# Gate and up products of a SwiGLU layer as seven products of half-size blocks

## The chip, the cores and the metric

One core of a Trainium2 chip runs the whole program. The metric is device time in microseconds (us) of one execution; lower is better. TensorE does the matrix products, VectorE (DVE in the profile), ScalarE (ACT) and GpSimd (POOL) the elementwise work, SyncE (SP) issues the loads.

## The reference

Two pre-norm layers over 512 tokens of width 1024 in float32, each followed by a dense SwiGLU feed-forward of width 2816. Layer 0 mixes tokens with windowed attention, layer 1 with latent attention. The feed-forward is what the change concerns:

```python
def _swiglu(h, w_gu, w_down):
    g, u = jnp.split(h @ w_gu, 2, axis=-1)
    return (jax.nn.silu(g) * u) @ w_down

h = h + _swiglu(_rmsnorm(h, norm_ffn[i]), ffn_w_gu[i], ffn_w_down[i])
```

`h @ w_gu` is 512 x 1024 by 1024 x 5632 in each layer. Float32 accuracy is wanted throughout.

## The kernel before

**Data.** The stream lies transposed: `h`, `x_hi`, `x_lo` are 128 partitions x 8 blocks of the width x 512 tokens. To keep float32 accuracy every operand A is split as A = hi + lo, where hi is A rounded to the format `F32R` that TensorE takes, and lo the rest, rounded likewise; a product is three matmuls (`product`: lo·hi, hi·lo, hi·hi) added up in a PSUM bank. x is split once per layer. The weights are split as they arrive: GpSimd writes `w_hi` (`w_split_hi`, L530), VectorE the rest `w_lo` = `w_raw` - `w_hi` (`w_split_lo`, L2330).

**Feed-forward.** It has 22 pairs of a gate block and an up block of 128 columns, in two halves of 11 (`HALF`); each half first makes its 11 pairs of products and the hidden blocks f = silu(gate)·up (`f_hi`, `f_lo`), then runs 8 down blocks of 11 products each, added to `h`. A pair is 2 blocks x 8 width blocks x 3 = 48 matmuls with 512 columns moving. VectorE multiplies gate by the inverse norm `rs_t` (L2666), ScalarE takes silu (L1118), GpSimd multiplies by `rs_t` once more for the up part (L727), VectorE multiplies with up out of PSUM (`hid`, L2681), ScalarE rounds (`f_hi`, L1121), VectorE subtracts (`f_lo`, L2683).

**Order.** It is written out by hand for each engine; semaphores are the only order between engines (`w_ready` for a split weight block, `w_used` for one multiplied, `proj_free` for a bank read). Most pairs run in hardware loops (`Fori`). Weight blocks alternate between two slots, loaded by SyncE (`load`, `load_ffn`).

## Time and profile before

| what | value |
|---|---|
| median of 3 timed runs | 1155.4 us (1154.16 to 1155.7) |
| span of the profiled execution | 1153.3 us |
| TensorE busy | 1141.3 us, 99% of the span |
| VectorE / ScalarE / GpSimd busy | 607.6 / 334.1 / 460.7 us |
| moved by DMA | 97.81 MB, 85 GB/s mean |
| granted clock of TensorE | 0.998 of full, mean |

The profiled execution has no timed value of its own; its span, first to last instruction, is 2.1 us below the median of the timed runs. Busy time of an engine is the time with an instruction in it. Matmuls overlap their neighbours, so the start-to-start distance, not the duration, says what a matmul costs in a row of them. The idle time in square brackets names the engine whose signal ended the wait.

### The profile page before, as it was taken

The numbers are of one execution on the slowest core, as the hardware profiler recorded it, in microseconds if no ns is written. First come the engines' busy times: TensorE is split into PE (matmuls) and PEld (weight loads), VectorE is DVE, ScalarE is ACT, GpSimd is POOL, SyncE is SP. The second block draws the span as 40 slices with busy tenths as digits, with TensorE's granted clock in tenths as the row PEclk, the third lists the DMA queues.
The fourth block names the chain that finished last, engine by engine and source line by source line (L and its number), as shares of the span: only waits on it lengthen the run. The fifth ranks groups of instructions, "written<-read, shape, count | busy, mean of one in ns | idle before, by whom it ended". The sixth has DMA issues, their size and how long they took to land.

```text
span 1153.3 us, 17024 instructions
## 1 busy us (share of the span) xinstructions
PE 1141.3 (99%) x5674; PEld 957.3 (83%) x5674; DVE 607.6 (53%) x1036; ACT 334.1 (29%) x709; POOL 460.7 (40%) x487
## 2 busy tenths in 40 slices
PE   8999999999999999999999999999999999999997
PEld 8877688888888888888998888888888888888886
...
GB/s 193 111 37 38 37 80 99 96 91 94 116 100 74 104 96 91 113 100 97 84 40 39 19 20 37 37 110 92 106 94 98 118 80 87 95 106 91 126 76 73
DMA packets 175362, 97.81 MB, mean 85 GB/s; under 512 B 7880, under 2 KB 171216, under 8 KB 175312
## 3 DMA queue, kind: packets, MB, share of 16 engines
...
## 4 chain that ended last, share of the span: by engine, by line
PE 95%; DVE 2%; ACT 1%; DMA 1%; issue 0%; POOL 0%; SPq 0%; ACTq 0%; DVEq 0%
PE bank L1415 28%; PE bank L1419 28%; PE bank L1418 28%; PE bank L2082 2%; PE bank L2101 1%; PE bank L2104 1%; PE bank L1645 1%; PE bank L1629 1%; PE bank L1660 1%; PE bank L1661 1%; PE bank L2013 1%; DMA w_raw<-in_a_w_qkv 1%; ACT s_a L1006 0%; PE bank L1515 0%; PE bank L1851 0%
## 5 line engine op out<-in xcount | busy, mean ns | idle before, releaser
L2330 DVE TENSOR_TENSOR w_lo<-w_raw,w_hi 128x1024 fp32r<-128x1024 f32 (+3 forms) x139 | 189.2, 1362 | 280.4 <-POOL w_hi L530 280.4
L530 POOL TENSOR_SCALAR w_hi<-w_raw 128x1024 fp32r<-128x1024 f32 (+3 forms) x147 | 166.3, 1131 | 411.6 <-PE bank L1419 401.5
L1415 PE MATMUL bank<-x_hi,w_lo 128*128 128x512 f32 x744 | 290.8, 391 | 0.0
L1419 PE MATMUL bank<-x_hi,w_hi 128*128 128x512 f32 x744 | 289.7, 389 | 0.0
L1418 PE MATMUL bank<-x_lo,w_hi 128*128 128x512 f32 x744 | 289.5, 389 | 0.0
L1419 PEld LDWEIGHTS bank<-x_hi,w_hi 128*128 128x128 f32 x744 | 139.6, 188 | 29.1
L1418 PEld LDWEIGHTS bank<-x_lo,w_hi 128*128 128x128 f32 x744 | 139.7, 188 | 28.9
L1415 PEld LDWEIGHTS bank<-x_hi,w_lo 128*128 128x128 f32 x744 | 139.7, 188 | 28.5
L1415 PE MATMUL bank<-f_hi,w_lo 128*128 128x512 f32 (+1 forms) x363 | 139.7, 385 | 0.0
L1419 PE MATMUL bank<-f_hi,w_hi 128*128 128x512 f32 (+1 forms) x363 | 138.9, 383 | 0.0
L1418 PE MATMUL bank<-f_lo,w_hi 128*128 128x512 f32 (+1 forms) x363 | 138.9, 383 | 0.0
L727 POOL TENSOR_TENSOR gate_s<-gate_s,rs_t 128x512 f32<-128x512 f32 x44 | 56.7, 1288 | 114.2 <-ACT gate_s L1118 114.2
L1118 ACT ACTIVATE gate_s<-gate_t 128x512 f32<-128x512 f32 x44 | 27.8, 631 | 251.9 <-DVE gate_t L2666 251.9
L1121 ACT ACTIVATE f_hi<-hid 128x512 f32 (+1 forms) x44 | 27.8, 632 | 214.1 <-DVE hid L2681 214.1
L2631 DVE TENSOR_TENSOR h<-h,bank 128x512 f32<-128x512 f32 (+1 forms) x40 | 27.5, 688 | 112.5 <-PE bank L1419 109.0
L1418 PEld LDWEIGHTS bank<-f_lo,w_hi 128*128 128x128 f32 x363 | 68.2, 188 | 13.2
L1419 PEld LDWEIGHTS bank<-f_hi,w_hi 128*128 128x128 f32 x363 | 68.2, 188 | 13.3
L1415 PEld LDWEIGHTS bank<-f_hi,w_lo 128*128 128x128 f32 x363 | 68.2, 188 | 13.2
L812 POOL TENSOR_SCALAR s_b<-s_b,stat 128x512 f32<-128x512 f32 x64 | 44.9, 709 | 60.8 <-DVE stat L2624 60.6
L544 POOL TENSOR_TENSOR ss<-ss,sq 128x512 f32<-128x512 f32 x27 | 49.9, 1848 | 32.8 <-ACT sq L924 32.7
L2683 DVE TENSOR_TENSOR f_lo<-hid,f_hi 128x512 f32 (+1 forms) x44 | 30.5, 693 | 42.9 <-ACT f_hi L1121 42.9
L2976 DVE TENSOR_TENSOR bpt_lo<-bank,bpt_hi 128x512 fp32r<-128x512 f32 x64 | 42.5, 683 | 9.3 <-ACT bpt_hi L1248 9.1
...
## 6 DMA issues: line engine op xcount, KB each, us to landing
w_raw<-in_ffn_w_gu SPq DMA_DIRECT2D x88, 512.0 KB, 3.8
...
w_raw<-in_a_w_qkv SPq DMA_DIRECT2D x10, 512.0 KB, 4.6
w_raw<-in_a_w_o SPq DMA_DIRECT2D x8, 512.0 KB, 3.5
w_raw<-in_b_w_o SPq DMA_DIRECT2D x8, 512.0 KB, 3.7
...
x_n<-in_x SPq DMA_DIRECT2D x4, 512.0 KB, 5.6
```

The source lines that it names most:

```text
L530: pool.tensor_scalar(split_part(w_hi, s, cols, kv), raw_part(s, cols, kv), 1.0, 1.0, ALU.mult, ALU.mult) \
L544: pool.tensor_tensor(n.ss[:], n.ss[:], n.sq[:, b, :], ALU.add).then_inc(ss_ready, 1)
L727: pool.tensor_tensor(gate_s[:], gate_s[:], rs_t[:], ALU.mult).then_inc(silu_rs_ready, 1)
L812: pool.tensor_scalar(view, view, stat[:, 2, u % 8:u % 8 + 1], 1.0, ALU.mult, ALU.mult) \
L1118: act.activation(gate_s[:], gate_t[:], ACT.Silu).then_inc(silu_ready, 1)
L1121: act.activation(f_hi[:, j, :], hid[:], ACT.Copy).then_inc(f_hi_ready, 1)
L1415: first = pe.matmul(o, ll, rh, start=start, stop=False)
L1418: pe.matmul(o, lh, rl, start=False, stop=False)
L1419: return pe.matmul(o, lh, rh, start=False, stop=stop)
L2330: dve.tensor_tensor(split_part(w_lo, s, cols, kv), raw_part(s, cols, kv), f(split_part(w_hi, s, cols, kv)), ALU.subtract) \
L2683: dve.tensor_tensor(f_lo[:, j, :], hid[:], f(f_hi[:, j, :]), ALU.subtract).then_inc(f_ready, 1)
L2976: dve.tensor_tensor(bpt_lo[:, hd % 2, i, :], banks[3 + u % 2][:], f(bpt_hi[:, hd % 2, i, :]), ALU.subtract).then_inc(pt_free, 1)
```

## The change

Of the 22 pairs in a layer the first two stay as they were. Each of the other 20 is computed as a 2 x 2 block product: the width of 1024 is cut into two halves of 4 blocks (`HK`), the 512 tokens into two halves of 256 columns (`HT`), and the third division is gate against up. With weight blocks A11, A12 (gate, low and high width), A21, A22 (up) and x blocks X11 (low width, early tokens) and so on, the seven products are Strassen's in Winograd's form:

- weight sums S1 = A21 + A22, S2 = S1 - A11, S3 = A11 - A21, S4 = A12 - S2, made for each pair by GpSimd (`sums_12`, `sums_43`);
- x sums T1 to T4, made once a layer while the attention's output product runs (`t_first`, `t_last`, `t_high`, `t_low`);
- seven products of 4 blocks each, 7 x 4 x 3 = 84 matmuls with 256 columns moving (`seven`), two of them with x itself, twice each over halves, the others with sums.

Sums and blocks are split into hi and lo in four groups: G0 = A11, A12 (1024 columns), G1 = S1, S2 (1024), G2 = A22 (512), G3 = S4, S3 (1024). ScalarE makes the hi parts (`group_hi`), VectorE the lo parts (`group_lo`). The products share banks; ScalarE copies partial results from PSUM to SBUF between them (`take_product`, four a pair, 256 columns each) and TensorE adds later products on top of what stands in the bank (`add_product`). VectorE finishes gate and up with three additions (`late_gate`, `rest_of_unit`); up now lies in SBUF, no longer in PSUM, when `hid` is multiplied. Raw weights of a pair come into one slot of 1 MB (`load_raw`) as two transfers of 512 KB, two such slots alternate. The loops are unrolled. Down products are as before, in the new slots.

```diff
+            def load_raw(layer, c0, r, cols, *parts):
+                if r >= 2:
...
+                        sp.wait_ge(g_ready, 4 * unit_of(past // RAW_LAYER, j) + 4)
...
+                for i, src in enumerate(parts):
...
+                    sp.dma_start(dst, src).then_inc(raw_in[r % 2], 16)
# GpSimd
+            def sums_12(layer, j):
...
+                pool.wait_ge(raw_in[r % 2], raw_landed(r))
+                if u:
+                    pool.wait_ge(g_ready, 4 * (u - 1) + 2)
...
+                pool.tensor_tensor(s12[:, 0:QUART], a21, a22, ALU.add).then_inc(s12_ready, 1)
+                pool.wait_ge(s12_ready, 2 * u + 1)
+                pool.tensor_tensor(s12[:, QUART:2 * QUART], s12[:, 0:QUART], a11, ALU.subtract).then_inc(s12_ready, 1)
+            def sums_43(layer, j):
...
+                if u:
+                    pool.wait_ge(g_ready, 4 * (u - 1) + 4)
+                pool.tensor_tensor(s43[:, QUART:2 * QUART], a11, a21, ALU.subtract).then_inc(s43_ready, 1)
+                pool.wait_ge(s12_ready, 2 * u + 2)
+                pool.tensor_tensor(s43[:, 0:QUART], a12, s12[:, QUART:2 * QUART], ALU.subtract).then_inc(s43_ready, 1)
# ScalarE, each pair j
+                    if j > 2 and j > j0:
+                        take_product(layer, j - 1, 3)
+                    group_hi(layer, j, 3)
+                    take_product(layer, j, 0)
+                    if j > 2 and j > j0:
+                        silu(layer, j - 1)
+                    if j + 1 < j1:
+                        group_hi(layer, j + 1, 0)
+                    take_product(layer, j, 1)
+                    take_product(layer, j, 2)
+                    if j > j0:
+                        f_high(layer, j - 1)
+                    if j + 1 < j1:
+                        group_hi(layer, j + 1, 1)
+                        group_hi(layer, j + 1, 2)
+            def take_product(layer, j, which):
+                if which == 0 and u:
+                    act.wait_ge(c_ready, 3 * u)
+                act.wait_ge(m_done, 7 * u + (1, 3, 4, 7)[which])
# TensorE, each pair
+                pe.wait_ge(g_ready, 4 * u + 1)
+                one(main[:, 0:HT], 0, 0, xs(0, early))
+                one(apart[:, 0:HT], 0, 1, xs(HK, early))
...
+                pe.wait_ge(g_ready, 4 * u + 2)
+                one(side[:, 0:HT], 1, 0, ts(0))
+                pe.wait_ge(m_read, 4 * u + 1)
+                one(main[:, 0:HT], 1, 1, ts(1), start=False)
+                pe.wait_ge(g_ready, 4 * u + 3)
+                one(apart[:, HT:T], 2, 0, ts(3))
+                pe.wait_ge(g_ready, 4 * u + 4)
+                pe.wait_ge(m_read, 4 * u + 2)
+                one(side[:, 0:HT], 3, 0, xs(HK, late), start=False)
+                pe.wait_ge(m_read, 4 * u + 3)
+                one(main[:, 0:HT], 3, 1, ts(2), start=False)
# VectorE
+            def group_lo(layer, j, g):
...
+                dve.wait_ge(g_hi_ready, 4 * u + g + 1)
+                dve.tensor_tensor(G_LO[g], group_raw(r, g), f(G_HI[g]), ALU.subtract).then_inc(g_ready, 1)
+            def late_gate(layer, j):
...
+                dve.tensor_tensor(gate_t[:, HT:T], u2_m5[:, 0:HT], banks[3 * (u % 2) + 1][:, 0:HT], ALU.add) \
+                    .then_inc(c_ready, 1)
+            def rest_of_unit(layer, j):
...
+                dve.tensor_tensor(hid[:, HT:T], m1_u3[:, HT:T], u2_m5[:, HT:T], ALU.add).then_inc(c_ready, 1)
+                dve.tensor_tensor(gate_up[:, :, 0:HT], m1_u3[:].rearrange("p (c n) -> p c n", c=2),
+                                  banks[3 * (u % 2) + 2][:].rearrange("p (c n) -> p c n", c=2), ALU.add) \
+                    .then_inc(c_ready, 1)
+                dve.wait_ge(c_ready, 3 * u + 3)
+                dve.tensor_tensor(gate_t, gate_t, rs_t[:], ALU.mult).then_inc(gate_ready, 1)
```

VectorE, within a half's pairs. Before, one turn of the loop (one pair):

```order
387 L2330 TENSOR_TENSOR w_lo_58<-w_raw_54,w_hi_56 128x1024 [waits w_hi_ready]
388 L2666 TENSOR_TENSOR gate_t<-bank,rs_t 128x512 [waits silu_ready,w_used]
389 L2330 TENSOR_TENSOR w_lo_59<-w_raw_55,w_hi_57 128x1024 [waits w_hi_ready]
390 L2681 TENSOR_TENSOR hid<-bank,gate_s 128x512 [waits f_ready,silu_rs_ready,w_used]
391 L2683 TENSOR_TENSOR f_lo<-hid,f_hi 128x512 [waits f_hi_ready]
```

The changed kernel, one pair at the same place in the second half (`u_m` is `u2_m5`, `m_u` is `m1_u3`, `s_126` is `s12`, `s_127` is `s43`; `gate_up` holds gate and `hid`):

```order
501 L2937 TENSOR_TENSOR x_lo<-s_127,x_hi 128x4x256 [waits g_hi_ready]
502 L2937 TENSOR_TENSOR w_lo_58<-raw_125,w_hi_56 128x1024 [waits g_hi_ready]
503 L2969 TENSOR_TENSOR gate_up<-gate_up,gate_s 128x512 [waits silu_rs_ready]
504 L2974 TENSOR_TENSOR f_lo<-gate_up,f_hi 128x512 [waits f_hi_ready]
505 L2937 TENSOR_TENSOR g_lo<-s_126,g_hi 128x1024 [waits g_hi_ready]
506 L2937 TENSOR_TENSOR w_lo_59<-raw_125,w_hi_57 128x512 [waits g_hi_ready]
507 L2945 TENSOR_TENSOR gate_up<-u_m_123,bank 128x256 [waits silu_ready,m_read,m_done]
508 L2953 TENSOR_TENSOR gate_up<-m_u_122,u_m_123 128x256 [waits f_ready,m_read]
509 L2954 TENSOR_TENSOR gate_up<-m_u_122,bank 128x2x256
510 L2958 TENSOR_TENSOR gate_up<-gate_up,rs_t 128x512 [waits c_ready]
```

Before, three of the five instructions of a pair took both inputs from SBUF (387, 389, 391), the other two took one from a bank. Now eight of ten take both from SBUF, and only rows 507 and 509 take one from a bank. The lo parts of G0, G1 and G2 made here are those of the next pair, that of G3 is this pair's.

GpSimd at the same place. Before:

```order
199 L727 TENSOR_TENSOR gate_s<-gate_s,rs_t 128x512 [waits silu_ready]
200 L530 TENSOR_SCALAR w_hi_57<-w_raw_55 128x1024 [waits w_used,w_in1]
201 L530 TENSOR_SCALAR w_hi_56<-w_raw_54 128x1024 [waits w_used,w_in0]
202 L727 TENSOR_TENSOR gate_s<-gate_s,rs_t 128x512 [waits silu_ready]
203 L530 TENSOR_SCALAR w_hi_57<-w_raw_55 128x1024 [waits w_used,w_in1]
```

The changed kernel, one pair:

```order
404 L835 TENSOR_TENSOR s_126<-raw_121 128x512 [waits g_ready,raw_in0]
405 L837 TENSOR_TENSOR s_126<-s_126,raw_121 128x512 [waits s12_ready]
406 L853 TENSOR_TENSOR gate_s<-gate_s,rs_t 128x512 [waits silu_ready]
407 L846 TENSOR_TENSOR s_127<-raw_121 128x512 [waits g_ready]
408 L848 TENSOR_TENSOR s_127<-raw_121,s_126 128x512 [waits s12_ready]
```

The two roundings of weights have gone to ScalarE, and four sums of two inputs stand in their place; `gate_s` waits behind the first two sums, which wait for the lo part of G1 (row 505 of VectorE).

## Rows read from the trace of the kernel before

**Rows 1.** The page: busy time by engine, then the chain that ended last
```profile
PE 1141.3 (99%) x5674; PEld 957.3 (83%) x5674; DVE 607.6 (53%) x1036; ACT 334.1 (29%) x709; POOL 460.7 (40%) x487
...
PE 95%; DVE 2%; ACT 1%; DMA 1%; issue 0%; POOL 0%; SPq 0%; ACTq 0%; DVEq 0%
```

**Rows 2.** Busy time by stretch: the gate and up products, layer 0, first half
```profile
core 0: us, PE busy (x) PEld busy (x) DVE busy (x) ACT busy (x) POOL busy (x), PEclk, DMA share, GB/s
212.00:307.00 95.00, 95.00 (x421) 78.67 (x420) 37.70 (x43) 11.38 (x18) 30.61 (x27) 1.00 0.36 105
```

**Rows 3.** Timeline of one pair: start us, us, engine line op [idle, releaser]
```profile
248.31 0.69 DVE L2666 TENSOR_TENSOR gate_t<-bank,rs_t 128x512 f32<-128x512 f32 x1
249.09 0.63 ACT L1118 ACTIVATE gate_s<-gate_t 128x512 f32<-128x512 f32 x1 [4.74 <-DVE gate_t L2666]
249.86 1.29 POOL L727 TENSOR_TENSOR gate_s<-gate_s,rs_t 128x512 f32<-128x512 f32 x1 [2.81 <-ACT gate_s L1118]
...
252.60 1.23 DVE L2330 TENSOR_TENSOR w_lo<-w_raw,w_hi 128x1024 fp32r<-128x1024 f32 x1 [3.61 <-POOL w_hi L530]
253.75 0.69 DVE L2681 TENSOR_TENSOR hid<-bank,gate_s 128x512 f32<-128x512 f32 x1
254.60 0.63 ACT L1121 ACTIVATE f_hi<-hid 128x512 f32 x1 [4.88 <-DVE hid L2681]
...
259.18 0.69 DVE L2666 TENSOR_TENSOR gate_t<-bank,rs_t 128x512 f32<-128x512 f32 x1
```

**Rows 4.** Timeline of TensorE at the program's end, 256-column products
```profile
1139.04 0.28 PE L1419 MATMUL bank<-f_hi,w_hi 128*128 128x256 f32 x1
...
1140.83 0.28 PE L1419 MATMUL bank<-f_hi,w_hi 128*128 128x256 f32 x1
```

**Rows 5.** By tile: ns min/median/max, first and last start; the last by line: mean ns
```profile
L2330 DVE TENSOR_TENSOR w_lo<-w_raw,w_hi x139: 1218/1228/2302, 31.1 to 1129.3; 128x1024 fp32r<-128x1024 f32 x102, 128x1408 fp32r<-128x1408 f32 x32, 128x1344 fp32r<-128x1344 f32 x4, 128x1152 fp32r<-128x1152 f32 x1
...
L633 POOL TENSOR_TENSOR ot_lo<-oa_sum,ot_hi x15: 728/732/738, 68.6 to 147.9; 128x256 fp32r<-128x256 f32 x15
...
L2529 DVE TENSOR_TENSOR ot_lo<-oa_sum,ot_hi x1: 425/425/425, 150.1 to 150.1; 128x256 fp32r<-128x256 f32 x1
...
L1397 ACT ACTIVATE sq<-h_fin 128x256 f32<-128x256 f32 x2 | 0.8, 416 | 2.6 <-DVE h_fin L2739 2.6
```

**Rows 6.** Timelines of VectorE and GpSimd where the two overlap
```profile
159.86 1.22 DVE L2330 TENSOR_TENSOR w_lo<-w_raw,w_hi 128x1024 fp32r<-128x1024 f32 x1 [1.60 <-POOL w_hi L530]
160.07 2.16 POOL L544 TENSOR_TENSOR ss<-ss,sq 128x512 f32<-128x512 f32 x1 [0.24 <-ACT sq L924]
161.00 1.78 DVE L2354 SCALAR_TENSOR_TENSOR x_lo<-h,gains,x_hi 128x512 fp32r<-128x512 f32 x1
...
208.94 1.29 POOL L727 TENSOR_TENSOR gate_s<-gate_s,rs_t 128x512 f32<-128x512 f32 x1
209.01 2.30 DVE L2330 TENSOR_TENSOR w_lo<-w_raw,w_hi 128x1024 fp32r<-128x1024 f32 x1 [1.15 <-POOL w_hi L530]
...
509.28 1.63 DVE L2330 TENSOR_TENSOR w_lo<-w_raw,w_hi 128x1408 fp32r<-128x1408 f32 x1 [0.74 <-POOL w_hi L530]
510.33 1.73 POOL L544 TENSOR_TENSOR ss<-ss,sq 128x512 f32<-128x512 f32 x1 [1.15 <-ACT sq L924]
510.83 1.78 DVE L2354 SCALAR_TENSOR_TENSOR x_lo<-h,gains,x_hi  x1
```

**Rows 7.** Timeline of VectorE in the down products, two blocks' additions
```profile
507.85 0.69 DVE L2631 TENSOR_TENSOR h<-h,bank 128x512 f32 x1 [2.79 <-PE bank L1419]
...
515.34 0.69 DVE L2631 TENSOR_TENSOR h<-h,bank 128x512 f32 x1 [2.74 <-PE bank L1419]
```

**Rows 8.** DMA issues: KB each, median us to landing
```profile
w_raw<-in_ffn_w_gu SPq DMA_DIRECT2D x88, 512.0 KB, 3.8
```

**Rows 9.** Timeline of VectorE at the start of the first feed-forward
```profile
194.66 1.23 DVE L2330 TENSOR_TENSOR w_lo<-w_raw,w_hi 128x1024 fp32r<-128x1024 f32 x1 [6.88 <-POOL w_hi L530]
```

More of the change, by code:

```diff
@@ L58 @@
 C_FFN1 = C_WOB + KD
-C_END = C_FFN1 + 2 * C_HALF
+C_END = C_FFN1 + C_FFN
 W_COLS = KD * P
@@ L121, with unit_of, raw_unit, raw_down @@
 LRS_KV, LRS_Q = 6, 7
+FFN_UNITS = FB - 2
+UNITS_0 = HALF - 2
+HK, HT = KD // 2, T // 2
+QUART = HK * P
+RAW_LAYER = FFN_UNITS + 2 * KD
+def unit_of(layer, j):
+    return FFN_UNITS * layer + j - 2
+def raw_unit(layer, j):
+    return RAW_LAYER * layer + (j - 2 if j < HALF else j - 2 + KD)
+def raw_down(layer, half, m):
+    return RAW_LAYER * layer + (UNITS_0 + m if half == 0 else FFN_UNITS + KD + m)
+def raw_is_unit(r):
+    at = r % RAW_LAYER
+    return at < UNITS_0 or UNITS_0 + KD <= at < FFN_UNITS + KD
+def raw_landed(r):
+    return sum(32 if raw_is_unit(i) else 16 for i in range(r % 2, r + 1, 2))
+def down_block(c0, half, m):
+    return c0 + 4 + KD * half + m
+def landed(c2):
+    return 16 * (c2 + 1 - (KD if 2 * c2 >= C_LAT else 0))
 def two_pi_parts():
@@ L1804, in ffn_half, with add_product @@
+            def add_product(o, lh, ll, rh, rl):
+                for a, b in ((ll, rh), (lh, rl), (lh, rh)):
+                    last = pe.matmul(o, a, b, start=False, stop=False, skip_group_check=True)
+                return last
             def ffn_half(layer, half, n, fin=None):
-                c2 = ((C_FFN0, C_FFN1)[layer] + half * C_HALF) // 2
-                u0 = (U_FFN0, U_FFN1)[layer] + half * C_HALF
-                j0 = (2 * layer + half) * HALF
+                c0, u0 = (C_FFN0, C_FFN1)[layer], (U_FFN0, U_FFN1)[layer]
@@ L1852, in turn, with last_pair @@
                     last.then_inc(pt_done, 1)
-                down(0, 0, first=True)
-                down(0, 1)
+                for m in range(KD - 1 if fin else KD):
+                    down(m)
+                    if fin and m:
+                        turn(m - 1)
                 if fin:
-                    turn(0, 0)
-                with pe.Fori(1, KD // 2 - (fin is not None)) as i:
-                    down(i, 0)
-                    if fin:
-                        turn(2 * i - 2, 1)
-                    down(i, 1)
-                    if fin:
-                        turn(2 * i, 0)
-                if fin:
-                    last_pair(c2 + HALF + KD // 2 - 1, down, turn)
-            def last_pair(c2, down, turn):
+                    last_pair(down_block(c0, half, LAST), turn)
+            def last_pair(b, turn):
                 def block_half(half, ks):
@@ new lines, in wo_phase, with down_lo @@
+            def wo_phase(n, c0):
+                for m in range(KD):
+                    add_to_h(None if m == 2 else m % 2, m, c0 + m + 1)
+                    if m:
+                        w_split_lo((c0 + m + 2) // 2, m % 2, W_COLS)
+                    if m >= 6:
+                        t_low(n, m - 6)
+                    split_x_lo(n, m)
+                    if m >= 5:
+                        t_last(n, m - 5)
+                t_low(n, 2)
+            def down_lo(layer, c0, half, m):
+                b, r, cols = down_block(c0, half, m), raw_down(layer, half, m), W_DOWN
+                dve.wait_ge(w_hi_ready, b + 1)
+                dve.tensor_tensor(w_lo[m % 2][:, 0:cols], raw_slot[r % 2][:, 0:cols], f(w_hi[m % 2][:, 0:cols]),
+                                  ALU.subtract).then_inc(w_ready, 1)
```

540 lines of the change are left out of this document (358 added, 182 removed).

## The prediction

> **What bounds the kernel now.** I read the page first. TensorE is busy for 99% of the span and 95% of the chain that ended last is its own [rows 1]. In the gate and up products it has work for all of 95.00 us, while VectorE has 37.70 and GpSimd 30.61, and the granted clock is 1.00, the 2.4 GHz level [rows 2]. So a change pays here if it shortens TensorE's stream, as long as the other engines keep up. The timeline of one pair gives the price of a pair: the same gate multiplication starts at 248.31 and at 259.18, which is 10.87 us for 48 matmuls, 0.2265 us each with 512 columns [rows 3]. Every other engine idles in between, and for most of that time.
>
> **TensorE's part of the change.** The end of the program has a run of the new shape: from 1139.04 to 1140.83 lie 15 steps between 256-column products of the same three-pass pattern, 0.1193 us each [rows 4]. A pair becomes 84 of them, 10.02 us instead of 10.87. If nothing else mattered, 40 pairs would give 40 x 0.85 = 34 us back. That is the prize. The down products keep their price: 7.49 us from one block's addition to the next [rows 7].
>
> **What a pair asks of the others.** VectorE: three lo parts of 1024 columns, one of 512, three full multiplications or subtractions (gate by norm, hid, f_lo), one addition of 256 and one of 512 (one input in PSUM each), one addition of 256 from SBUF. Alone these take 1.23, 0.69 and 0.42 us [rows 3, 5]: 3 x 1.23 + 0.69 x 5 + 0.42 x 2 = 8.0 us of 10.02. GpSimd: four sums and gate_s, 5 x 1.29 = 6.4 us [rows 3]. ScalarE: no row shows a 1024-column instruction; 256 columns take 0.42 [rows 5] and 512 take 0.63 [rows 3], so I estimate 1.06 by the same slope. Three of these, 0.63 three times (A22, silu, f_hi), four copies at 0.42: 6.8 us. Each engine alone fits under 10.02.
>
> **VectorE and GpSimd together do not fit.** The rows where they meet show it. The subtraction w_lo ends at 161.08; GpSimd's two-input addition, started at 160.07, ends at 162.23, 1.15 us after it, though such an instruction takes 1.29 alone; VectorE's x_lo, started at 161.00, ends at 162.78, 0.55 after that. At 509.28 the same three do the same: ends 510.91, 512.06 (1.15 later), 512.61 (0.55 later). At 208.94 GpSimd comes first and ends at 210.23; w_lo, which takes 1.23 alone, needs 2.30 and ends at 211.31, 1.08 after it [rows 6]. One waits for all of the other. All of these VectorE instructions take both inputs from SBUF. In before this costs nothing, since there is slack; here the two engines must share the time. The Trainium skill, page "SBUF — State Buffer", section "Who interferes with whom", says the same of this pair of engines, and adds that a VectorE instruction with one input in PSUM does not contend. It speaks against this change, and if it failed here the first rival below would hold.
>
> A pair has five such GpSimd instructions, 5 x 1.15 = 5.75 us, and eight of VectorE: 3 x 1.08, five of 512 less the one in PSUM makes four x 0.55, one of 256 at about 0.28 (half of 0.55): 5.72 us. Together 11.5 us, already over the 10.87 of before. That is the floor of a pair if they take turns without a gap.
>
> **The turn-taking in order.** I walk the fixed order with these durations and 0.1 us for a signal (0.09 from gate_t's end to silu, 0.14 from silu to gate_s [rows 3]). Zero is the end of the lo part of G1. VectorE: lo of G2 to 0.60. GpSimd's S1 to 1.75. hid's first addition 2.03. S2 3.18, beside which VectorE adds gate and up out of PSUM (to 2.63). Gate by norm 3.73. Lo of G3 4.81, beside which ScalarE takes silu (to 4.46). gate_s 5.96. Lo of the next G0 7.04 (its hi part ready at 5.6). S3 8.19. hid 8.74. ScalarE's f_hi 9.47, S4 beside it to 9.89. f_lo 10.44, ScalarE's hi part of G1 10.54. Lo of G1 from 10.64 with its full 1.23: 11.9 us. So a pair takes 11.9 us in a long run, 0.4 over the floor. TensorE fits inside: the third product starts at 0, the fourth must wait for ScalarE's copy of the first, which waits for the addition at 2.63, so it starts at 3.2; four products of 1.43 end at 8.9, the next pair's first two at 11.8. TensorE then idles some 1.8 us of each pair.
>
> **The ends of each half.** A half has a head start, since G0 to G2 of its first pair are made beside the down products (or the first pairs) before. The lo of the second pair's G1 ends 8.6 us after the first pair's start (fourth product at 5.7, hi part, lo part); the third pair's 12.3 later, since the first pair's last product (10.0) must be copied before the additions; then 11.9 each. After the last pair's G1 there are no sums, but two roundings of down weights, and the last f_lo comes at about 17.2: gate and up added at 12.9 behind the second down block's lo part, silu 13.6, gate_s 15.0, hid 15.7, f_hi 16.4, f_lo 17.2. The down block needs it for its eleventh step, 30 x 0.2265 = 6.8 us after it starts. For 9 pairs: 8.6 + 12.3 + 6 x 11.9 + 17.2 - 6.8 = 102.7; for 11: 126.5. Before: 97.8 and 119.6. The difference is 4.9 + 6.9 a layer, 23.6 in all.
>
> **The small parts.** The x sums stand in the attention output product. VectorE was idle for 6.88 us before its next weight there [rows 9], but GpSimd gets two 256-column sums a block (0.73 each [rows 5]) beside sums of squares, and the two meet again. At the layer's start S1 to S4 of the first pair stand ahead of gate_s. From nothing to 3 us a layer; I take 1.5, 3 us in all, since the idle is long and the chain short. The raw weights: the next load waits for the lo part of G3 at 4.8; a 512 KB transfer lands in 3.8 us [rows 8]; the second behind it at twice that at most, 7.6, and at nothing more at least. S1 needs them 7.1 us after the wait ends, so anything from no wait to 0.5 a pair; I take none. The tables of sines and the frequencies move beside a down block, which leaves VectorE over 2 us idle in rows of before [rows 7]; nothing. Unrolled code: rows 4 are unrolled code and show no wait; nothing, up to 5 us for the rest.
>
> **Sum.** 1153.3 + 23.6 + 3 = 1179.9 for the profiled span. What lies around the span is 2.1 us (1155.4 less 1153.3), left as it is: 1182 us, 2.3% slower.
>
> **Rivals.**
> - *They do not block each other.* Against it stand all of rows 6; for it, that those VectorE rows meet GpSimd once or twice in 10 us, never in a long alternation, and that 256-column or strided operands appear in none. VectorE's own ring is then: lo of G2, three additions, gate by norm 2.6, silu and hi of G0 to 4.4, lo 5.7, hid 6.4, f_hi 7.1, hi of G1 8.2, lo 9.5 us, under 10.02. TensorE is the bound again: 1155.4 - 34 + 3 = 1124 us. This one ends on the other side. It decides at a ring of about 11.0: under that the head starts make the halves shorter than before. Chance 13%.
> - *The ring is longer.* Each pass has some ten handings-over; at 0.2 instead of 0.1, or with one instruction going first in the wrong place (GpSimd's S4 before f_lo is such a place, 0.5 to 1.1 us), it is 12.8 to 13. A layer has 14 long-run pairs (6 + 8), 28 in all: 28 x 1.0 = 28 us more, 1210 us. For it: signals took 0.09 to 0.16 us [rows 3]. Against it: much of it lies beside work. Chance 17%.
> - *The raw weights come late*, at 8 us and more for both transfers, 0.5 to 1 us a pair: 1195 to 1210. For it: 1 MB is asked for at once. Against it: the DMA engines were busy 0.36 of the time [rows 2]. Chance 5%.
> - *The floor*: 11.5 and a better start, 28 x 0.4 = 11 us less, 1171, or, if the pair's signals hide wholly and a sum overlaps with its neighbour, down to no change. Chance of no change 5%.
>
> My forecast as it stands, 1168 to 1196, has 60%. The range that holds 8 in 10 reaches down to near no change, 1158, and up to 1216. What a measurement of this kernel can tell from no change is about 0.2%, 2.3 us. Faster by more: the first rival, and a little for halfway cases, 15%. No change: 5%. Slower: 80%.
>
> **What would show it.** Start to start of silu in the long run of a half: 11.9 if I am right, 10.0 in the first rival. VectorE's 1024-column subtractions and GpSimd's sums: a good part of them at 1.9 to 2.4 us instead of 1.23 and 1.29. TensorE idle before the first matmul of the fourth product, released by ScalarE's copy, and before the third, released by the lo part of G1. TensorE's step in a product: 0.119; if it is 0.13 or more, the prize itself is gone. ScalarE's 1024 columns: 1.06. I am wrong if TensorE is still busy without gaps through the pairs.

## The result and the profile after

1214.6 us (1213.3 to 1215.8, 4 runs) against 1155.5 (1154.2 to 1155.7): ratio 1.0515, interval 1.050 to 1.053. The kernel got 59 us slower where I forecast 27, so the loss is 2.2 times the forecast one. The direction was right, and the measured time lies inside the stated range (1158 to 1216), close to its upper end.

The page of the kernel after, busy time and chain, against [rows 1]:

```profile
PE 1133.1 (93%) x7114; PEld 1011.2 (83%) x7114; DVE 863.2 (71%) x1260; ACT 537.8 (44%) x1053; POOL 672.8 (55%) x583
...
PE 51%; DVE 30%; ACT 7%; issue 7%; POOL 4%; DMA 1%; DVEq 0%; ACTq 0%; POOLq 0%
```

TensorE's share of the chain that ended last fell from 95% to 51%, and VectorE now has 30% of it. Against the pair of [rows 3], one pair in a long run of the kernel after, first VectorE, then GpSimd (both: start us, us, instruction, [idle before, releaser]):

```profile
456.86 0.68 DVE L2937 TENSOR_TENSOR w_lo<-raw,w_hi 128x512 fp32r<-128x512 f32 x1
457.46 0.42 DVE L2945 TENSOR_TENSOR gate_up<-u_m,bank 128x256 f32<-128x256 f32 x1
457.79 1.19 DVE L2953 TENSOR_TENSOR gate_up<-m_u,u_m 128x256 f32<-128x256 f32 x1
458.90 0.67 DVE L2954 TENSOR_TENSOR gate_up<-m_u,bank 128x512 f32<-128x512 f32 x1
459.61 1.04 DVE L2958 TENSOR_TENSOR gate_up<-gate_up,rs_t 128x512 f32<-128x512 f32 x1
460.57 1.21 DVE L2937 TENSOR_TENSOR x_lo<-s,x_hi 128x1024 fp32r<-128x1024 f32 x1
462.30 1.72 DVE L2937 TENSOR_TENSOR w_lo<-raw,w_hi 128x1024 fp32r<-128x1024 f32 x1 [0.52 <-ACT w_hi L1292]
463.94 1.77 DVE L2969 TENSOR_TENSOR gate_up<-gate_up,gate_s 128x512 f32<-128x512 f32 x1
466.42 1.00 DVE L2974 TENSOR_TENSOR f_lo<-gate_up,f_hi 128x512 fp32r<-128x512 f32 x1 [0.70 <-ACT f_hi L1317]
467.36 1.23 DVE L2937 TENSOR_TENSOR g_lo<-s,g_hi 128x1024 fp32r<-128x1024 f32 x1
468.50 0.68 DVE L2937 TENSOR_TENSOR w_lo<-raw,w_hi 128x512 fp32r<-128x512 f32 x1
```

```profile
457.08 1.61 POOL L835 TENSOR_TENSOR s<-raw 128x512 f32<-128x512 f32 x1 [1.86 <-DVE g_lo L2937]
458.77 1.33 POOL L837 TENSOR_TENSOR s<-s,raw 128x512 f32<-128x512 f32 x1
461.40 1.54 POOL L853 TENSOR_TENSOR gate_s<-gate_s,rs_t 128x512 f32<-128x512 f32 x1 [1.29 <-ACT gate_s L1309]
462.90 2.27 POOL L846 TENSOR_TENSOR s<-raw 128x512 f32<-128x512 f32 x1
465.13 1.74 POOL L848 TENSOR_TENSOR s<-raw,s 128x512 f32<-128x512 f32 x1
```

The lo part of G2 starts at 456.86 and at 468.50: 11.65 us a pair (11.9 forecast, 10.87 before). hid's addition of 256 columns takes 1.19 instead of 0.42, S3 2.27 instead of 1.29: each waits for the other engine's instruction. The two at L2945 and L2954, with one input in PSUM, keep their 0.42 and 0.67 though S1 (L835) and S2 (L837) run beside them. The Trainium skill, page "SBUF — State Buffer", section "Who interferes with whom", names these two cases (two SBUF inputs contend, one does not), and the trace agrees.

TensorE, same pair, and its longest waits of the first half of layer 0:

```profile
458.33 0.28 PE L1643 MATMUL bank<-t_lo,g_hi 128*128 128x256 f32 x1
458.45 0.28 PE L1644 MATMUL bank<-t_hi,g_hi 128*128 128x256 f32 x1
460.04 0.39 PE L2079 MATMUL bank<-t_hi,g_lo 128*128 128x256 f32 x1 [1.32 <-ACT m_u L1301]
...
201.71 0.79 PE L1640 MATMUL bank<-x_hi,w_lo 128*128 128x512 f32 x1 [3.12 <-DVE w_lo L2594]
220.49 0.36 PE L1640 MATMUL bank<-x_hi,w_lo 128*128 128x256 f32 x1 [4.30 <-DVE w_lo L2937]
```

TensorE takes the seven products in the order A11·X11, A12·X21, S1·T1, S2·T2, A22·T4, S4·X22, S3·T3; three of them take x itself, where the section on the change says two. The step in a product is 0.12, as in [rows 4]. The wait before the fourth product, 1.3 us, is where I put it; the one that I had named before the third did not come. 28 waits before the fourth make 34.0 us:

```profile
PE bank L2079 <- ACT m_u L1301: 34.0, 28, 1.4
PE bank L1640 <- DVE f_lo L2974: 13.5, 4, 4.1
PE bank L1640 <- DVE w_lo L2937: 12.6, 4, 4.3
PE bank L1640 <- DVE w_lo L2594: 9.4, 5, 3.1
```

(Waits of TensorE over the whole span: total us, times, longest.) The second and third line are the ends and the starts of the halves, the fourth the attention output product and pairs 0 and 1. None of the four is in the kernel before. Together they are 69.5 us, of which 35.5 lie outside the long run of pairs. I compared the stages by the starts of VectorE's additions to h. Layer 0, before and after: attention output 32.0 and 36.8; from there to the last down block of the first half 180.75 and 196.2; second half 179.5 and 191.1. That is +4.8, +15.4, +11.6; layer 1 has +4.0, +16.5, +8.6 (the last one up to the addition of the seventh of the eight down blocks). The forecast had 1.5 for the start and 4.9 and 6.9 for the halves.

The first pair's start, GpSimd, VectorE and the granted clock by stretch:

```profile
210.71 1.28 POOL L835 TENSOR_TENSOR s<-raw 128x512 f32<-128x512 f32 x1 [7.77 <-DVE t_lo L2910]
...
215.81 1.28 POOL L853 TENSOR_TENSOR gate_s<-gate_s,rs_t 128x512 f32<-128x512 f32 x1
```

```profile
209.35 1.22 DVE L2910 TENSOR_TENSOR t_lo<-s,t_hi 128x1024 fp32r<-128x1024 f32 x1
...
217.13 0.69 DVE L2967 TENSOR_TENSOR gate_up<-bank,gate_s 128x512 f32<-128x512 f32 x1 [5.65 <-POOL gate_s L853]
218.51 0.69 DVE L2974 TENSOR_TENSOR f_lo<-gate_up,f_hi 128x512 fp32r<-128x512 f32 x1 [0.70 <-ACT f_hi L1317]
219.12 1.22 DVE L2937 TENSOR_TENSOR w_lo<-raw,w_hi 128x1024 fp32r<-128x1024 f32 x1
```

```profile
203.00:206.00 3.00, 3.00 (x8) 2.32 (x8) 2.22 (x5) 0.68 (x1) 0.00 (x0) 0.50 0.00 0
...
221.00:224.00 3.00, 3.00 (x18) 3.00 (x17) 3.00 (x3) 0.38 (x1) 2.30 (x2) 0.57 0.00 0
```

(The third group: stretch, busy time of TensorE, its weight loads, VectorE, ScalarE and GpSimd, then the granted clock, DMA share and GB/s.) t_lo of the fourth block stands behind rs_t's copy, so GpSimd idles for 7.77 us; then its four sums go ahead of gate_s of pair 0, VectorE waits 5.65 for that, and G0 of pair 2, queued behind it, comes 4.30 too late. The wait of 3.12 before it has another source. The last of the activations' sums and their split stand beside the weight split of pair 0, VectorE first:

```profile
198.46 1.23 DVE L2910 TENSOR_TENSOR t_lo<-s,t_hi 128x1024 fp32r<-128x1024 f32 x1 [1.13 <-ACT t_hi L1263]
199.60 2.06 DVE L2594 TENSOR_TENSOR w_lo<-w_raw,w_hi 128x1024 fp32r<-128x1024 f32 x1
```

```profile
198.75 1.83 POOL L623 TENSOR_SCALAR w_hi<-w_raw 128x1024 fp32r<-128x1024 f32 x1 [1.69 <-PE bank L1644]
200.55 1.69 POOL L802 TENSOR_TENSOR s<-m_u 128x256 f32<-128x256 f32 x1
```

w_hi takes 1.83 instead of 1.05, w_lo 2.06 instead of 1.22, and TensorE starts 0.05 behind w_lo's end. After both waits the granted clock of this execution is lower for a few us: 0.50, which is the 1.2 GHz level, and 0.57, a mean over both levels.

### The profile page after: what moved, and what is told of

It is laid out like the page before. It is cut to its first block, busy times and chain, and to the rows that moved or that the text cites. A ratio compares the mean times of both kernels' runs of the same rounds, so it can differ in the third digit from the quotient of the medians.

```text
span 1213.9 us, 18428 instructions
## 1 busy us (share of the span) xinstructions
PE 1133.1 (93%) x7114; PEld 1011.2 (83%) x7114; DVE 863.2 (71%) x1260; ACT 537.8 (44%) x1053; POOL 672.8 (55%) x583
## 4 chain that ended last, share of the span: by engine, by line
PE 51%; DVE 30%; ACT 7%; issue 7%; POOL 4%; DMA 1%; DVEq 0%; ACTq 0%; POOLq 0%
PE bank L1640 13%; PE bank L1644 13%; PE bank L1643 13%; DVE w_lo L2937 7%; DVE gate_up L2969 5%; DVE f_lo L2974 3%; DVE gate_up L2953 3%; DVE gate_up L2958 3%; ACT w_hi L1292 3%; PE bank L2346 2%; ACT f_hi L1317 2%; DVE gate_up L2954 2%; DVE g_lo L2937 1%; PE bank L2365 1%; PE bank L2368 1%
## 5 line engine op out<-in xcount | busy, mean ns | idle before, releaser
L1640 PE MATMUL bank<-x_hi,w_lo 128*128 128x256 f32 (+1 forms) x424 | 136.8, 323 | 21.4 <-DVE w_lo L2937 12.6
L1640 PE MATMUL bank<-f_hi,w_lo 128*128 128x512 f32 (+1 forms) x363 | 141.6, 390 | 13.5 <-DVE f_lo L2974 13.5
L1643 PE MATMUL bank<-x_lo,w_hi 128*128 128x256 f32 (+1 forms) x424 | 134.9, 318 | 0.0
L1644 PE MATMUL bank<-x_hi,w_hi 128*128 128x256 f32 (+1 forms) x424 | 134.8, 318 | 0.0
L835 POOL TENSOR_TENSOR s<-raw 128x512 f32<-128x512 f32 x40 | 64.1, 1601 | 104.0 <-DVE g_lo L2937 74.0
L2937 DVE TENSOR_TENSOR w_lo<-raw,w_hi 128x1024 fp32r<-128x1024 f32 x80 | 93.8, 1173 | 22.7 <-ACT w_hi L1292 22.7
L1640 PEld LDWEIGHTS bank<-x_hi,w_lo 128*128 128x128 f32 x424 | 83.8, 198 | 28.5 <-issue 14.2
L1292 ACT ACTIVATE w_hi<-raw 128x1024 fp32r<-128x1024 f32 x80 | 66.6, 832 | 79.3 <-PE bank L1644 79.3
L2895 DVE TENSOR_TENSOR h<-h,bank 128x512 f32<-128x512 f32 x40 | 27.4, 686 | 94.6 <-PE bank L1644 91.1
L1644 PEld LDWEIGHTS bank<-x_hi,w_hi 128*128 128x128 f32 x424 | 84.2, 199 | 4.7
L1643 PEld LDWEIGHTS bank<-x_lo,w_hi 128*128 128x128 f32 x424 | 84.0, 198 | 3.8
L846 POOL TENSOR_TENSOR s<-raw 128x512 f32<-128x512 f32 x40 | 86.0, 2150 | 0.0
L1644 PEld LDWEIGHTS bank<-f_hi,w_hi 128*128 128x128 f32 x363 | 68.9, 190 | 13.8
L2079 PE MATMUL bank<-t_hi,g_lo 128*128 128x256 f32 x160 | 48.3, 302 | 34.0 <-ACT m_u L1301 34.0
```

Of the source, the lines that this page charges most:

```text
L835: pool.tensor_tensor(s12[:, 0:QUART], a21, a22, ALU.add).then_inc(s12_ready, 1)
L846: pool.tensor_tensor(s43[:, QUART:2 * QUART], a11, a21, ALU.subtract).then_inc(s43_ready, 1)
L1292: act.activation(G_HI[g], group_raw(r, g), ACT.Copy).then_inc(g_hi_ready, 1)
L1640: first = pe.matmul(o, ll, rh, start=start, stop=False)
L1643: pe.matmul(o, lh, rl, start=False, stop=False)
L1644: return pe.matmul(o, lh, rh, start=False, stop=stop)
```

## The experiments

Times are medians; the interval is that of the ratio to before. "After" is 1214.6. Before was timed beside each run and stayed within 1154.5 and 1155.3, so that differences of 1 us between the runs below say nothing.

**e1_nosums.** Is it GpSimd's reads? Four lines of this kind:

```
- pool.tensor_tensor(s12[:, 0:QUART], a21, a22, ALU.add).then_inc(s12_ready, 1)
+ pool.memset(s12[:, 0:QUART], 0.0).then_inc(s12_ready, 1)
```

> GpSimd's four weight sums of each pair are replaced by writes of zero to the same 512 columns: same place, same signals, but they read nothing and are shorter. What is left out: the sums S1 to S4. Theory (VectorE and GpSimd take turns at their SBUF reads, and this sets the 11.65 us of a pair): a pair falls to TensorE's own 10.0 to 10.1 us, the wait before the fourth product is gone, VectorE's 1024-column subtractions take 1.23 again; with the shorter start 1160 to 1172 us in all. Rival B (the fourth product's wait for ScalarE's copy sets it, the copy's buffer being free only after VectorE's addition): VectorE's first addition comes 0.76 us sooner, a pair takes 10.9, 1185 to 1190 us. Rival C (the order of signals alone): 11.5 or more, 1210 us.

1148.3 us, 0.995 (0.993 to 0.997). That is below the 1160 to 1172 that I expected. Silu to silu is 10.08 (422.92, 433.00), and TensorE waits before the first pair of a half but nowhere in the pairs behind it:

```profile
422.92 0.64 ACT L1309 ACTIVATE gate_s<-gate_up 128x512 f32<-128x512 f32 x1 [0.31 <-DVE gate_up L2958]
433.00 0.63 ACT L1309 ACTIVATE gate_s<-gate_up 128x512 f32<-128x512 f32 x1 [0.32 <-DVE gate_up L2958]
```

The sums cost 66 us, the 34.0 of the long run's waits among them. More fell away than I had counted: the waits for f_lo went from 13.5 to 2.8 and those for the first pair of a half from 12.6 to 6.5. But a memset takes 0.53, so reads and lateness are still mixed; e6 parts them.

**e2_twobuf.** Is it the copies' single buffer? `m1_u3` doubled, alternating by pair; ScalarE's first copy waits for `c_ready` of two pairs ago.

> The buffer that ScalarE's copy of the first product goes to is doubled, so the fourth product need not wait for VectorE's additions of the pair before. Theory (turn-taking): the pair stays at 11.65 us within 0.1, TensorE's idle time moves from the fourth product to the third, which then waits for the lo part of G1; within 3 us of 1214.6. Rival B (the buffer sets the pair): 10.1 us a pair, 1160 us.

1215.8, 1.053 (1.051 to 1.055). Still 11.65 a pair; TensorE's wait moved to the sixth product (1.14), behind ScalarE's second copy, and not to the third as I had written. Doubling the buffer gives nothing: TensorE waits for the ring of VectorE, GpSimd and ScalarE.

**e3_fold.** One GpSimd instruction less a pair, one VectorE instruction longer:

```
- dve.tensor_tensor(gate_t, gate_t, rs_t[:], ALU.mult).then_inc(gate_ready, 1)
+ dve.tensor_tensor(gate_up[:], gate_up[:], rs_t[:].unsqueeze(1).to_broadcast([P, 2, T]), ALU.mult).then_inc(gate_ready, 1)
```

GpSimd's `scale_gate` returns at once for the 20 pairs.

> GpSimd's gate_s product with the inverse norm is dropped for the 20 pairs; VectorE multiplies gate and up together by it, 1024 columns instead of 512. Turn-taking theory: 1.15 us of GpSimd's reads go, 0.53 of VectorE's come, 0.6 less a pair: 11.0 us, and 28 long-run pairs give 17 us, 1195 to 1200 in all. Rival B: additions come at the same time, the pair stays at 11.65. Rival C (signals): two hand-overs and 1.3 us go from the chain and 0.5 comes, 10.6 us a pair, 1185.

1239.2, 1.073 (1.071 to 1.076): slower by 25 us, and my expectation wrong. Silu to silu is 12.40. VectorE's multiplication takes 1.57 instead of 1.04, and with gate_s out of the way S3 and S4 follow at once:

```profile
458.37 1.29 POOL L846 TENSOR_TENSOR s<-raw 128x512 f32<-128x512 f32 x1 [2.30 <-DVE x_lo L2938]
459.61 2.28 POOL L848 TENSOR_TENSOR s<-raw,s 128x512 f32<-128x512 f32 x1
```

S4 stands ahead of hid (460.66, 1.78). By my prices the sum of the turns fell by 0.6, yet a pair takes 0.75 more. This run changes two things, the longer multiplication and the order; e10 drops gate_s without the longer multiplication, and e11 then changes the order.

**e4_start.** `t_low(3)` ahead of `take_rs_t`, and `scale_gate(0)` ahead of `sums_43(2)`.

> Order at the start of each layer's feed-forward only: VectorE makes the last lo part of the x sums before it waits for the inverse norm, GpSimd multiplies gate_s of pair 0 after two of the first four sums, not after all. Theory (TensorE's 4.3 us idle before its first product comes from this queueing, and its slow clock of about 2 us after it from the idleness): the idle falls under 1 us and the clock stays at its upper level there: 4 to 6 us a layer, 1203 to 1207 us. Rival (the first product waits for something else, the hi part of G0 or the weights' load): within 2 us of 1214.6.

1209.4, 1.048 (1.046 to 1.050), 5.2 us less, short of the 1203 to 1207 that I expected. The wait before pair 2 falls from 4.30 to 1.13, but the first wait of the long run comes earlier (241.87 instead of 258.37): the long run takes back a part of the head start. The two edits were not run apart, but in e1, which leaves both places as they were and only shortens the four sums, this wait falls to 1.22.

**e5_half.** `group_lo(layer, HALF, 0)` and `(.., 1)` ahead of the last block's `add_to_h` in half 0.

> The lo parts of G0 and G1 of pair 11 stand on VectorE ahead of the last down block's addition to h in the first half of each layer, instead of behind it. If TensorE's wait of 2.0 us at the second half's start (387.48 in the changed kernel) and the fall of the granted clock behind it (0.79 to 0.87 at 385 to 395) come from that place in VectorE's queue, the wait goes to under 0.5 us, the clock stays near 1.00 there, and 2.0 + 1.7 us a layer are saved, 7 us in all, less what the long run of pairs takes back, since its period of 11.65 us is set by VectorE and GpSimd: between 1206 and 1213 us. Rival: the second half's start is bound by the sums of GpSimd (S1 of pair 11 behind w_hi of the last down blocks), then nothing is gained and the wait moves to the third product: 1214 to 1216 us.

1210.1, 1.047 (1.045 to 1.049), 4.6 us less; the 2.0 us wait is gone.

**e6_busy.** As e1, but each sum is three memsets with a wait of GpSimd on itself between them, as long as a sum.

> Each of GpSimd's four sums a pair is replaced by three memsets (512, 512 and 256 columns) one after the other, with a wait of GpSimd on itself between them: GpSimd is busy for 1.3 to 1.6 us a sum as before, gives its signals as late as before, and reads nothing from SBUF. The sums are left out of the computation. Theory of turns at the SBUF reads: the period of a pair in the long run stays near the 10.1 us of the kernel with one memset a sum, up to 10.5 if a signal now comes late, and the whole takes 1146 to 1160 us. Rival: what GpSimd costs is its own time and the lateness of its signals: the period comes back to 11.3 to 11.7 and the whole to 1200 to 1215 us. If writes alone already contend, VectorE's 1024-column subtractions show 1.9 to 2.4 us again.

1161.6, 1.006 (1.005 to 1.008), 1.6 above the theory's range and far from the rival's 1200. Rows of VectorE and of GpSimd:

```profile
437.46 1.22 DVE L2950 TENSOR_TENSOR x_lo<-s,x_hi 128x1024 fp32r<-128x1024 f32 x1
...
444.91 0.42 DVE L2958 TENSOR_TENSOR gate_up<-u_m,bank 128x256 f32<-128x256 f32 x1
445.88 0.43 DVE L2966 TENSOR_TENSOR gate_up<-m_u,u_m 128x256 f32<-128x256 f32 x1 [0.55 <-ACT m_u L1314]
...
447.54 1.22 DVE L2950 TENSOR_TENSOR x_lo<-s,x_hi 128x1024 fp32r<-128x1024 f32 x1
```

```profile
439.78 2.90 POOL L832 MEMSET s<- 128x512 f32 x6
444.50 3.02 POOL L832 MEMSET s<- 128x512 f32 x6 [1.82 <-DMA raw<-in_ffn_w_gu]
```

GpSimd is busy for 1.45 a sum, more than the real 1.29, yet a pair takes 10.08 (437.46 to 447.54) and hid's addition its 0.43. So it is that GpSimd reads, not how long it is busy. 53 of the 66 us of e1 go away with the reads alone; the other 13 come back with the longer memsets, 7.6 of them as waits before the first pairs (14.1 instead of 6.5).

**e7_fill.** `for _ in range(20): pe.matmul(banks[3][:, 0:P], ident[:], ident[:], start=True, stop=True)` ahead of pair 2.

> Twenty fp32 products of the 128x128 identity with itself, into a bank that nobody reads, stand on TensorE ahead of the first of the seven products of pair 2 in each layer, where it waits 4.3 us for VectorE. They should run inside that wait. If the lower granted clock at 221 to 227 (0.57 and 0.86) comes from this idleness, the clock is near 1.00 there and 1 to 1.7 us a layer are saved: 1211 to 1213 us. But the long run behind it is bound by VectorE and GpSimd; if TensorE's head start only runs into its first idle (258) earlier, then nothing is gained: 1214 to 1216 us. I give the second 60%, since with the earlier first product the long run took back most of what the start had gained.

1213.4, 1.051 (1.049 to 1.053), not to be told from the change as made. The granted clock was 1.00 at 220 to 230, but in this execution also at 200 to 210, behind the same 3.12 us wait as before. So this run can't price the lower level. The executions of one kernel say more. e9's four took 1198.8, 1201.8, 1205.4 and 1207.0 us at a mean granted clock of 0.992, 0.988, 0.985 and 0.982: 8.2 us for 0.010. The same goes with it in e14 (1170.4 at 0.996, 1176.9 at 0.989), but not in e15 (1150.0 at 0.996, 1150.1 at 0.993). That the clock alone makes the difference is not shown.

**e8_mix.** A model: pairs 4, 7, 10, 12, 15, 18, 21 get memsets and seven more matmuls; with the edits of e4 and e5.

> A model of a mixed kernel: 7 of 20 pairs a layer (4, 7, 10, 12, 15, 18, 21) have memsets of the same columns in place of the four sums, which leaves the sums out of the computation there, and get seven more 256-column matmuls, so that TensorE needs 10.85 us for them as for a pair of before; the other 13 are unchanged. It has the two edits of the start (t_low and scale_gate earlier) and of the second half's start (lo parts of G0 and G1 ahead of the last addition). The theory: three pairs ask VectorE and GpSimd for 2 x 11.5 + some 9 = 32 us and TensorE for 2 x 10.02 + 10.87 = 30.9, with room for the ring to catch up: the period over three pairs is 31 to 33 us. Against the kernel before (32.6): no gain to a gain of 1.7 us per three pairs, and the wo phases and tails still cost 5 to 8 us a layer. 1150 to 1175 us; I take 1160. Rival: a pair without sums does not give the ring time back (the wait for ScalarE's copy stays 1.3 us in all other pairs): 2 x 11.65 + 10.9 = 34.2 per three pairs, 1180 to 1190 us.

1173.5, 1.016 (1.015 to 1.018), at the upper end of the theory's range and below the rival's. Three pairs take 33.3 us where the theory had 31 to 33.

**e9_noxsum.** The activations' sums cut to two columns (`t_first`, `t_last`).

> The sums of the normalised activations (four operations of 256 columns for each of four blocks a layer, two on GpSimd and two on VectorE) become two-column ones that read next to nothing; they are left out of the computation. Their split into hi and lo parts stays. This prices what they cost the attention output phase (+4.5 us a layer against before) and the start of the first pair. If they are the cause: from the last attention-output addition but seven to the last the phase takes 33 to 34 us instead of 36.8 (before 32.0), the wait of 3.12 us falls under 1.5, and the whole is 6 to 14 us below 1214.6: 1200 to 1208. Rival: t_lo and ScalarE's copies cost the phase its time, not the sums: 1211 to 1214.

1203.6, 1.043 (1.041 to 1.045), 11 us less. The attention output phase is at 32.65 (152.14 to 184.79) and the waits of 1.28 and 3.12 are gone, while the wait before pair 2 stays at 4.33. Before, the phase had 32.03, so the sums made 4.2 of its +4.8.

**e10_late.** The up half's norm behind the down product; GpSimd's `scale_gate` gone:

```
+ dve.tensor_tensor(gate_t[:, cols], bank, rs_t[:, cols], ALU.mult)
+ dve.tensor_tensor(dst, src, gate_t[:, cols], ALU.add)     # in place of dst = h + bank
```

> The norm of the up half is applied behind the down product instead of by GpSimd on gate_s: gate_s is no longer scaled (one GpSimd instruction of 512 columns less a pair), and VectorE multiplies each down block by rs_t as it takes it out of PSUM (16 more instructions of 512 columns a layer, beside the down products, where VectorE idles). The result is the same. If only the sum of the turns counted, a pair would take 11.65 - 1.15 = 10.5 us and the whole 28 x 1.15 = 32 us less: 1182 to 1188. By the walk in order, S4 now takes the turn between S3 and hid, since nothing holds it back: hid ends as late as before, the period stays 11.5 to 11.9, and the whole is 1212 to 1222. I expect the second.

1211.2, 1.049 (1.048 to 1.051), 0.8 below the second's range, and 11.88 a pair: one turn less makes a pair of the long run no shorter. The 3.4 us come with shorter waits for f_lo (5.7 instead of 13.5) and before the first pairs (9.0 instead of 12.6). **e11_lateh** adds a wait ahead of S4, in all but the first pairs of the halves:

```
+ if j > 2 and j - 1 != HALF - 1 and j != HALF:
+     pool.wait_ge(hid_ready, u - 1)
```

> As the one before, and GpSimd's S4 waits until hid is done, so that it runs beside ScalarE's f_hi. By the walk: lo of G3 to 4.81, S3 5.96, lo of G0 7.04, hid 7.6, S4 8.75 beside f_hi 8.3, f_lo 9.3, ScalarE's hi of G1 9.4, lo of G1 10.6: a period of 10.5 to 10.8 instead of 11.65, and 28 x 1.0 = 28 us less, 1182 to 1192 in all. If the place of a sum in the order does not matter, this is the same as the one before. If another ring closes (ScalarE's three parts of 1024 columns, the raw weights), it stays over 11.2.

1184.9, 1.026 (1.024 to 1.028), 26 us less for one wait, and 11.03 a pair, over the 10.5 to 10.8 of the walk. The same two operations, in e10 and then in e11:

```profile
435.54 2.28 POOL L851 TENSOR_TENSOR s<-raw,s 128x512 f32<-128x512 f32 x1
...
436.59 1.78 DVE L2983 TENSOR_TENSOR gate_up<-gate_up,gate_s 128x512 f32<-128x512 f32 x1
```

```profile
438.94 0.68 DVE L2985 TENSOR_TENSOR gate_up<-gate_up,gate_s 128x512 f32<-128x512 f32 x1
...
439.76 1.29 POOL L853 TENSOR_TENSOR s<-raw,s 128x512 f32<-128x512 f32 x1 [1.83 <-DVE gate_up L2985]
```

In e11 hid is alone and S4 starts beside ScalarE's f_hi, where VectorE has nothing to do. It ends beside f_lo, which takes 1.29 instead of 0.69, as the walk had it. S3 and S4 now start only at a signal, with nothing to wait out, and take their full 1.29 where the walk counted 1.15; that is most of what a pair takes over 10.6. The turns are the same in number.

**e12_starthalf** (e4 and e5 together), **e13_allout** (with the edits of e1 and e9 too, so that both kinds of sums are left out) and **e14_bestl** (e4, e5 and e11, the whole computation).

> The two edits of the start (t_low ahead of take_rs_t, gate_s of pair 0 ahead of S3 and S4 of pair 2) and the one of the second half's start, together. They touch different places, so that I expect the sum of what each gave: 5.2 + 4.6 = 9.8 us below 1214.6, 1203 to 1207 us. If the long run takes back what the start gives, as it did in part, 1206 to 1210.

> All named costs are taken away at once: GpSimd's sums of weights are memsets, the sums of activations nearly nothing (both left out of the computation), and the edits of the start and of the second half's start are in. If the ledger is complete, what is left of the loss is the tails (0.7 us four times), the first pair's start and some lower clock, and TensorE's 34 us come through less 5 to 10: 1126 to 1132 us. If it stays above 1138, a cost of the seven products is not in the ledger.

> The whole computation, with the norm of the up half applied behind the down product, S4 held until hid is done, and the edits of the start and of the second half's start. If the gains add (29.7 and 10.9 us off 1214.6): 1174 us, 1171 to 1178. It stays slower than before, since a pair still takes 11.0 us against 10.87 and the attention output phase its 4.5 a layer.

1203.7 (1.040 to 1.044); 1130.2 (0.977 to 0.980); 1171.8 (1.013 to 1.019). All three are in their ranges: the costs add, and 25 of TensorE's 34 us are there once the named costs are gone.

**e15_mixl** is e14 with the model of e8.

> The kernel of e14_bestl with the model of plain pairs as in e8_mix (7 of 20 pairs a layer without sums of weights, which are left out of the computation there, and with seven more matmuls of 256 columns). Three pairs ask VectorE and GpSimd for 2 x 11.03 + 9 = 31 us and TensorE for 30.9: TensorE's waits in the long run should almost vanish, 26 x 0.85 = 22 us are its prize, and attention output (9 us), starts and tails (10 us) take nearly all of it: 1153 to 1164 us, I take 1159. Under 1150 it would point to a mixed kernel that beats before.

1150.1, 0.996 (0.995 to 0.997), 3 us below the range and 9 below what I took. It pointed to a mixed kernel that computes everything.

**e16_mixed** computes everything:

```
+ PLAIN = (2, 3, 7, 10, 11, 15, 18, 21)
...
+        g3_hi, g3_lo = region(scratch + 54 * 1024, [("g3_hi", [P, 2 * QUART], F32R), ("g3_lo", [P, 2 * QUART], F32R)])
```

A plain pair is computed as before, with 48 matmuls of 512 columns, its gate block in the tiles of G0 and its up block in those of G3. The activations' sums have moved from the attention output product to pairs 0 to 3. The norm behind the down product and the held S4 are those of e11.

> The whole computation. Pairs 2, 3, 7, 10, 11, 15, 18 and 21 of a layer are plain (48 products of 512 columns, gate block in the tiles of G0, up block in those of G3, no sums), the other 12 by seven products. G3 has tiles of its own, so that the activations stay whole. The sums of the activations stand beside pairs 0 to 3 instead of in the attention output phase. Norm of the up half behind the down product, S4 held until hid is done, lo part of G0 of pair 11 ahead of the last addition. By the ledger: TensorE's prize is 24 x 0.85 = 20.4 us; the attention output phase costs nothing more (the kernel without the sums of activations had it at 32.65 against 32.03 us), the halves end and begin with plain pairs, so that no wait for f_lo or G0 is left; runs of two or three seven-product pairs each lose at most 0.7 us to the ring, 16 x 0.3 = 5 us at most, and a few us go to lower clock and the longer path behind the last down block (0.7). 1155 - 20.4 + 3 to 8: 1138 to 1143 us. Rival: the activations' sums now disturb pairs 0 to 3 (GpSimd's and VectorE's turns beside the path of the norm), 3 to 5 us a layer: 1145 to 1150. Above 1155 the ledger is wrong.

1151.8, 0.998 (0.997 to 0.999): 0.2% faster than before, but 9 us over the range and 2 over the rival's. One wait a layer was left, 4.38 us before pair 2, with the clock at 0.57 in 210 to 215. **e17_mixed2** puts G0 of pair 2 ahead of silu (ScalarE) and of t_low and gate 1 (VectorE); **e18_mixed3** has six plain pairs a layer instead of eight.

> As e16_mixed, with the hi part of G0 of pair 2 ahead of silu of pair 0 on ScalarE and its lo part ahead of t_low and gate 1 on VectorE, and the last of the activations' sums one place later. TensorE's wait of 4.38 us before pair 2 goes under 0.3, and with it the stretch at a granted clock of 0.57 to 0.75 that follows it: 4.3 + 2 to 3 us a layer, 12 to 15 us in all: 1137 to 1140 us. If the wait only moves to the up block of pair 2 or to pair 3, it is 1143 to 1150.

> As e17_mixed2 with fewer plain pairs: 2, 3, 10, 11, 16 and 21 a layer, so 14 by seven products, in runs of 6, 4 and 4. TensorE's work is 4 x 0.85 = 3.4 us less. A seven-product pair takes 11.0 us in a long run and 10.0 while it has a head start; the run of 6 will end with some waits of 0.7 us. I expect 1.5 to 3.4 us less than e17_mixed2; if the run of 6 loses all of its gain and the last S4 stands late before the plain pair, the same as e17_mixed2 or 1 us more.

1141.8, 0.989 (0.987 to 0.991), and 1143.9, 0.990 (0.989 to 0.992). e17 missed its range by 2 us, since a wait of 1.43 stayed where I expected under 0.3. e18 is 2.1 us slower than e17 where I expected 1.5 to 3.4 less, or at worst 1 more. Of the kernels that compute everything e17 is the fastest, 13 us under before. Its page, its stretch of products (first half, layer 0) and its one wait there:

```profile
PE 1125.0 (99%) x6538; PEld 983.2 (86%) x6538; DVE 785.2 (69%) x1213; ACT 501.9 (44%) x957; POOL 477.8 (42%) x475
```

```profile
209.27 0.50 PE L1718 MATMUL bank<-x_hi,w_lo 128*128 128x512 f32 x1 [1.43 <-DVE gate_up L3068]
```

```profile
210.00:310.00 100.00, 99.96 (x638) 91.04 (x638) 70.97 (x77) 44.87 (x68) 35.97 (x22) 1.00 0.37 103
```

In e17's pairs TensorE has no wait over 0.24 (one, in layer 1). In e18 the run of six pairs has waits of 0.79 and 0.71 again: the ring sets in at the fifth.

## Why the prediction was right in sign and wrong in size

- **TensorE's part**: right, 0.12 a step; e13 shows 25 us of the prize.
- **VectorE and GpSimd take turns at the reads**: right, the step the forecast rests on (e1, e6, e11). 11.65 a pair against 11.9; 28 long-run pairs make this term 7 us too large. Set against the rows of the pair above, with zero at 456.94, the walk holds to 0.05 us at every step of VectorE and GpSimd down to f_lo (10.44 forecast, 10.48 measured). The rest lies in the lo part of G1, which starts at 10.42 and not at 10.64.
- **Order, not sum, sets the ring**: the walk in order was right, and foretold which way e10 and e11 went. 11.65 is near the "floor" of 11.5 too, but the sum of the turns does not explain the runs: e3 and e10 had less to take turns for and took 12.40 and 11.88 a pair.
- **"From nothing to 3 us a layer; I take 1.5" for the small parts** is the step that failed most. In its place the runs showed 16.2 us where the sum had 3 for both layers: 11.0 for the activations' sums (e9), which lengthen the instructions beside them and delay w_lo, and 5.2 for the order at the layer's start (e4), where S1 to S4 hold gate_s back and TensorE waits 4.30 before pair 2. By stages it is +4.8 and +4.0 in the attention output phase and a part of the first halves' excess. I had named both meetings and walked neither; I had walked the pair's ring only.
- **"G0 to G2 of its first pair are made beside the down products"** failed for the second halves: the hi parts of G0 and G1 were, the lo parts stood on VectorE behind the last addition (2.0 us wait; e5 gave 4.6).
- **The ends**: 17.2 less 8.9 less 6.8 leaves a wait of 1.5 us for f_lo; 2.9 to 4.1 were measured (13.5 for four, where the forecast had 6). Without gate_s on GpSimd they are 5.7 (e10). At the end of layer 0's first half GpSimd takes gate_s ahead of the first down block's rounding, and the second rounding waits for its transfer, which the forecast left out:

```profile
319.79 1.62 DVE L2930 TENSOR_TENSOR w_lo<-raw,w_hi 128x1408 fp32r<-128x1408 f32 x1 [2.52 <-POOL w_hi L822]
322.53 1.37 POOL L822 TENSOR_SCALAR w_hi<-raw 128x1408 fp32r<-128x1408 f32 x1 [2.77 <-DMA raw<-in_ffn_w_down]
```

- **Clock**: the sum had no term for it. The trace after has it at 0.50 to 0.86 behind the long waits. 1 less the granted clock, summed over stretches of 3 us of the whole span, is 14.9 us against 2.2 before, 5 of them in layer 0's first half; 12.7 is the most that it can cost. By e9's 8.2 us for 0.010, and the means of 0.985 to 0.989 against 0.998 before, it would be some 9 us, an estimate. In e9's profile the same sum is 9.5, so a part of it is in what e9 gave back.
- **Rivals**: no blocking is refuted. The longer ring did not come (11.65, not 12.8 to 13), though the time (1215) fell near its 1210. That nearness is luck, and so is it that the time lies inside the range, whose upper end was there for this rival. Late raw weights: GpSimd waited 9 times, 15.6 us in all, TensorE never for it.

The two profiled spans differ by 60.6 us. The stages give 8.8 to the attention output phases, 31.9 to the first halves, 20.2 to the second. The forecast for these was 3 (with the layer's start), 9.8 and 13.8. Of the 32.6 us by which 1182 fell short, the terms above make 18.3 (13.2 for the small parts, 4.6 for the second halves' starts and 7.5 for f_lo, less 7 for the long run). The clock has a share in the rest, which stays open. Counted the other way, the 60.6 and the 34 of the prize are 94.6 us to explain; TensorE's waits are 69.5 of them and the clock at most 12.7, and some 12 have no name in these rows.
